# A hybrid decoder step on one core: routing tables on column groups, router logits turned, and the choice of experts one turn later

## What is computed

```python
lg = (t @ w_rg) + b_rg                       # 4 group logits of a token
gsel = argmax(lg);  pg_sel = softmax(lg)[gsel]
le = ((t @ w_re) + b_re).reshape(-1, 4, 8)   # 32 expert logits
le_sel = le[token, gsel]
top_v, top_i = top_k(le_sel, 2)
gate = softmax(top_v) * pg_sel
y[token] += sum_k gate_k * expert[8 * gsel + top_i_k](t)   # SwiGLU, 1024 -> 256 -> 1024, 32 experts
```

## Time and profile before

| what | us |
|---|---|
| median of 3 runs | 1306.74 |
| lowest, highest | 1301.86, 1311.63 |
| profiled execution, its own time | 1308.17 |
| its span in the trace | 1306.4 |
| PE busy, DVE busy, ACT busy | 1193.0, 702.5, 317.9 |
| mean DMA rate over the span | 165 GB/s of HBM traffic |

### The profile page before, as it was taken

How to read it: one execution, slowest core, us unless ns; L and a number is a source line. 1 busy time by engine, 2 the same in 40 slices (tenths; PEclk the granted TensorE clock), 3 DMA queues, 4 the chain that set the end, 5 groups by cost and what they waited for, 6 DMA issues and landing times.

```text
span 1306.4 us, 17526 instructions
## 1 busy us (share of the span) xinstructions
PE 1193.0 (91%) x6401; PEld 615.3 (47%) x6401; DVE 702.5 (54%) x2179; ACT 317.9 (24%) x916; POOL 143.0 (11%) x159
## 2 busy tenths in 40 slices
PE   7989879999999998797999999999867999999895
PEld 3435545555555545453555665555532334333231
DVE  1219789999999997431345544554552254212121
ACT  1133435345345356220111111121100110110100
POOL 0000000000000001000000000000001233333232
PEclk9998889999999998898999999999877999999898
DMA  8871000300000004266111011000766998999993
GB/s 318 307 236 31 1 1 25 127 35 33 33 1 33 25 1 167 97 240 254 33 48 49 1 49 48 33 8 25 282 243 237 402 335 312 329 380 384 391 352 60
DMA packets 48913, 194.88 MB, mean 149 GB/s; under 512 B 12240, under 2 KB 15094, under 8 KB 36515
## 3 DMA queue, kind: packets, MB, share of 16 engines
q1 hardware_dynamic: 37883, 173.79, 34.5%
q0 software_dynamic: 10368, 17.87, 5.8%
q10 hardware_dynamic: 576, 2.10, 0.4%
HBM read 172.60 MB, written 42.36 MB: 165 GB/s over the span
## 4 chain that ended last, share of the span: by engine, by line
PE 48%; DVE 5%; DMA 4%; issue 2%; ACT 0%; POOL 0%; SPq 0%; POOLq 0%; DVEq 0%
PE bank L1355 10%; PE bank L830 9%; PE bank L1301 8%; PE bank L1362 6%; PE bank L1279 3%; PE bank L1239 2%; PE bank L1344 2%; DMA W<-in_w_exp_down 1%; PE bank L1319 1%; PE bank L1103 1%; DMA W<-in_w_mo 1%; PE bank L1162 1%; DMA W<-in_cache_mem_k 1%; PE bank L836 1%; DVE G L1790 1%
## 5 line engine op out<-in xcount | busy, mean ns | idle before, releaser
L830 PE MATMUL bank<-W,G 128*128 128x512 f32 (+1 forms) x768 | 314.2, 565 | 3.8 <-DVE G L1790 3.0
L1846 DVE SCALAR_TENSOR_TENSOR W<-W,dwT 128x128 f32<-128x128 f32 (+1 forms) x1048 | 271.7, 335 | 0.0
L830 PEld LDWEIGHTS bank<-W,G 128*128 128x128 f32 x768 | 145.4, 193 | 150.6 <-issue 147.2
L1355 PE MATMUL bank<-W 128*32 128x512 f32 x1344 | 175.0, 604 | 1.7 <-DVE W L2345 1.7
L1301 PE MATMUL bank<-W 128*128 128x512 f32 x256 | 113.3, 595 | 0.2 <-DVE W L2217 0.2
L1103 PE MATMUL bank<-W 128*128 128x512 f32 x256 | 112.8, 599 | 0.0
L2345 DVE TENSOR_TENSOR W<-bank,cvec 128x512 f32<-128x512 f32 x48 | 31.0, 686 | 140.1 <-PE bank L1344 140.1
L703 POOL TENSOR_SCALAR st<-st 128x1 f32<-128x1 f32 (+3 forms) x40 | 7.9, 198 | 898.5 <-DVE st L1944 441.7
L1355 PEld LDWEIGHTS bank<-W 128*32 128x32 f32 x1344 | 49.6, 112 | 108.6 <-issue 106.2
L1362 PE MATMUL bank<-W 128*32 128x512 f32 x672 | 87.3, 595 | 1.5 <-ACT W L1737 0.9
L1103 PEld LDWEIGHTS bank<-W 128*128 128x128 f32 x256 | 48.5, 192 | 58.7 <-issue 58.5
(11 more groups left out here) (351 smaller groups left out, 1576.1 us busy)
## 6 DMA issues: line engine op xcount, KB each, us to landing
W<-in_w_exp_gate SPq DMA_DIRECT2D x27, 1024.0 KB, 12.5
W<-in_w_exp_up SPq DMA_DIRECT2D x27, 1024.0 KB, 15.1
W<-in_w_exp_down SPq DMA_DIRECT2D x27, 1024.0 KB, 18.9
W<-in_cache_mem_k SPq DMA_DIRECT2D x8, 1024.0 KB, 5.5
W<-in_cache_mem_v SPq DMA_DIRECT2D x8, 1024.0 KB, 8.0
W<-in_w_in SPq DMA_DIRECT2D x4, 1792.0 KB, 25.1
G<-in_w_exp_gate SPq DMA_DIRECT2D x5, 1024.0 KB, 15.0
G<-in_w_exp_up SPq DMA_DIRECT2D x5, 1024.0 KB, 18.1
```

What stands on the lines that cost most here:

```text
L830: mm = pe.matmul(bank[0:rows, at:at + hi - lo], HT[:, c, 0:rows], w[:, c, lo:hi], start=(c == 0), stop=(c == DC - 1))
L1355: mm = pe.matmul(B[2 + par][lo:hi, :], HG[par][:, c, lo:hi], WGU[u][:, :, c, :], start=(c == 0), stop=(c == DC - 1), skip_group_check=True)
L1846: dve.scalar_tensor_tensor(y, src, w, y, ALU.mult, ALU.add).then_inc(M["conv_tap"], 1)
```

## The change

The router swaps its operands: 36 weight columns stationary, H3 moving, even chunks on array columns 0 to 63 and odd ones on 64 to 127. ACT copies both halves to LT, one more matmul with two stacked identities (PAIR) adds and turns them, inside the output projection. `route_table` puts (token, gate) x (choice 0, 1) on four column groups of 32. The choice of tiles 0 to 6 moves into the next turn, between Z3 and the score maxima; that of tiles 7 and 8 stays. In the last turns gates are made after rows and tables, block 0's index is cast from PSUM directly and gathered first, and the first `gate_up` starts on half of its rows.

```diff
+            "lt_ready": ("kT_ready", NT), "rtt_done": ("kT_done", NT), "r_odds": ("kn_ready", NT),
@@ POOL
-            pool.wait_ge(M["route_ready"], 1)
             pool.wait_ge(M["z3_out"], 16 * NT)
             for n in range(2):
+                pool.wait_ge(M["route_ready"], n + 1)
                 gather(idx_i[:, BLOCKS[n]:BLOCKS[n] + 1], zg_in[n], ZG[n])
@@ PE
             def route_rank(s4):
+                if s4:
+                    pe.wait_ge(M["r_acc"], AFTER["r_acc"] + s4)
+                    pe.matmul(B[3][:, 0:NE], ones, RA, start=True, stop=False)
                 pe.wait_ge(M["r_hot"], AFTER["r_hot"] + s4 + 1)
+                pe.matmul(B[3][0:n4, 0:NE], tri[0:n4, 0:n4], RM[0:n4, :], start=(s4 == 0), stop=True)
+            def table_part(bank, c, n4):
+                for k in range(2):
+                    lo = 64 * c + NE * k
+                    mm = pe.matmul(bank[lo:lo + NE, 64:64 + POS], RQ[0:n4, k, c, :], RR[0:n4, k, :], start=True, stop=True)
+            def router(s3):
+                for c in range(DC):
+                    if c % 4 == 0:
+                        pe.wait_ge(M["h3_ready"], AFTER["h3_ready"] + 2 * s3 + c // 4 + 1)
+                    lo = 64 * (c % 2)
+                    mm = pe.matmul(B[1][lo:lo + 36, 0:n3], wr[:, c, :], H3[:, c, 0:n3], start=(c < 2), stop=(c >= DC - 2))
+                mm.then_inc(M["rt_done"], 1)
+            def router_turn(s3):
+                pe.wait_ge(M["lt_ready"], AFTER["lt_ready"] + s3 + 1)
+                pe.matmul(B[1][0:n3, 256:292], LT[0:100, 0:n3], PAIR[0:100, :], start=True, stop=True).then_inc(M["rtt_done"], 1)
...
                     for c in range(DC):
+                        if c == 3 and turned >= 0:
+                            router_turn(turned)
                         mm = pe.matmul(B[2 + half][0:n2, :], OT2[:, c, 0:n2], w_mo[:, c, 512 * half:512 * half + 512])
...
                 if 0 <= s3 < NT:
+                    router(s3)
                 if 0 < s2 < NT:
-                    output_half(1)
+                    output_half(1, s3)
+                elif s3 == NT - 1:
+                    route_table(s4)
+                    router_turn(s3)
...
-            gate_up(tiles_of(0), 0).then_inc(M["gu_done"], 1)
+            gate_up(tiles_of(0), 0, 2).then_inc(M["gu_done"], 1)
@@ ACT
-                if 0 <= s4:
+                if s4 >= NT - 2:
                     gate_exp(s4)
                 if 0 <= s3 < NT:
                     act.activation(SQ2[0:n3, :], XB(s3)[0:n3, :], ACT.Square)
+                if 0 <= s4 < NT - 2:
+                    gate_exp(s4)
...
+                if 0 <= s3 < NT:
+                    act.wait_ge(M["rt_done"], AFTER["rt_done"] + s3 + 1)
+                    act.activation(LT[0:36, 0:n3], B[1][0:36, 0:n3], ACT.Copy)
+                    act.activation(LT[64:100, 0:n3], B[1][64:100, 0:n3], ACT.Copy).then_inc(M["lt_ready"], 1)
                 if 2 <= s1 + 1 < NT:
                     nxt = s1 + 1
@@ DVE, route_hot
-                link(dve.tensor_scalar(lg[:, 0:NG], lg[:, 0:NG], top[:, 0:1], None, ALU.subtract))
-                link(dve.tensor_scalar(sel, lg[:, NG:NG + EPG], og[:, 0:1], None, ALU.mult))
-                for g in range(1, NG):
-                    link(dve.scalar_tensor_tensor(sel, lg[:, NG + EPG * g:NG + EPG * g + EPG], og[:, g:g + 1], sel, ALU.mult, ALU.add))
+                link(dve.tensor_tensor(own.rearrange("p (g e) -> p g e", g=NG), lg[:, NG:36].rearrange("p (g e) -> p g e", g=NG), bc(og, EPG, 2), ALU.mult))
+                link(dve.tensor_reduce(sel, own.rearrange("p (g e) -> p e g", g=NG), X, ALU.add))
...
                 dve.tensor_tensor(RM[0:n, :], RO[0:n, 0, :], RO[0:n, 1, :], ALU.add).then_inc(M["r_hot"], 1)
+                link(dve.tensor_scalar(lg[:, 0:NG], lg[:, 0:NG], top[:, 0:1], None, ALU.subtract))
+                dve.tensor_tensor(lg[:, 4:5], top[:, 2:3], top[:, 1:2], ALU.subtract).then_inc(M["r_odds"], 1)
@@ DVE, last tile in route_add
                     dve.wait_ge(M["r_place"], AFTER["r_place"] + 1)
+                    dve.tensor_copy(idx_i[0:64, 0:1], B[3][0:64, 320:321])
+                    dve.tensor_copy(idx_i[64:128, 0:1], B[3][0:64, 320 + NR:321 + NR]).then_inc(M["route_ready"], 1)
                     link(place_blocks(T_TOK, B[3]))
+                    dve.tensor_copy(idx_i[:, 1:NR], T_TOK[:, 1:NR]).then_inc(M["route_ready"], 1)
@@ DVE, the loop
+            dve.memset(LT, 0.0)
+            dve.tensor_tensor(PAIR, ident[:, 0:36], ident[:, 64:100], ALU.add)
             for it in range(1, NT + 3):
...
                     dve.tensor_scalar(by_row(Z3[0:n3, :], DC), XB(s3)[0:n3, :], st[0:n3, 41:42], None, ALU.mult)
+                if 0 <= s4 < NT - 2:
+                    route_hot(s4)
...
+                if s2 >= NT and s4 < NT - 1:
+                    route_shares(s4)
                 if s4 >= 0:
                     route_add(s4)
+                if s4 == NT - 1:
+                    route_shares(s4)
+                    last_gates()
...
+                if 0 <= s2 < NT:
+                    add_x2(s2, 0)
                 if 0 <= s3 < NT:
-                    dve.wait_ge(M["rt_done"], AFTER["rt_done"] + s3 + 1)
+                    dve.wait_ge(M["rtt_done"], AFTER["rtt_done"] + s3 + 1)
...
-                if 0 <= s3 < NT:
+                if NT - 2 <= s3 < NT:
                     route_hot(s3)
                 if 0 <= s2 < NT:
+                    add_x2(s2, 1)
```

More of the change, by code:

```diff
@@ L57 @@
 HALVES = [k for k, b in enumerate(COLUMNS) if len(b) == 2 and b[1][3] == 2]
+assert BLOCKS[0] == 0 and [c[2:4] for c in COLUMNS[0]] == [(0, 2), (0, 2)]
 QUARTER = [[k for k, b in enumerate(COLUMNS) if len(b) == 2 and b[1][2:4] == (q, 1)] for q in range(5)]
@@ L1179, in last_gates @@
                 pe.wait_ge(M["r_gates"], NT)
-                for k in range(2):
-                    mm = pe.matmul(B[6][NE:2 * NE, 0:POS], RQ[:, k, 1, :], RR[:, k, :], start=(k == 0), stop=(k == 1))
-                mm.then_inc(M["r_gtable"], 1)
+                table_part(B[6], 1, 128).then_inc(M["r_gtable"], 1)
             for it in range(1, NT + 3):
@@ L1334, in _ @@
             pe.wait_ge(M["r_tt"], AFTER["r_tt"] + 2)
-            place(B[6], NE)
+            place(B[6], 2 * NE)
             def turn_rows(n, u, rows_in, count, banks=(0, 1)):
@@ L1350, in tiles_of, with gate_up @@
                 return [(PART * k, PART * k + PART, u) for k, u in enumerate(slots)]
-            def gate_up(tiles, par):
+            def gate_up(tiles, par, upper=0):
                 for c in range(DC):
+                    if c == DC // 2 and upper:
+                        pe.wait_ge(M["hg_ready"], upper)
                     for lo, hi, u in tiles:
@@ L2026, in _, with add_x2 @@
                     add_x1(NT - 1)
+            def add_x2(s2, half):
+                n2, xr, cols = rows_of(s2), XB(s2), slice(512 * half, 512 * half + 512)
+                dve.wait_ge(M["mo_done"], AFTER["mo_done"] + 2 * s2 + half + 1)
+                dve.tensor_tensor(xr[0:n2, cols], B[2 + half][held(s2, half), :], xr[0:n2, cols], ALU.add).then_inc(M["x2_ready"], 1)
             def route_hot(s3):
@@ L2084, in route_rows @@
                     link(a)
+                dve.wait_ge(M["r_exp"], AFTER["r_exp"] + s4 + 1)
+                link(dve.tensor_scalar(part[:, 2:3], part[:, 1:2], 1.0, part[:, 0:1], ALU.add, ALU.mult))
+                link(dve.reciprocal(gate[:, 0:1], part[:, 2:3]))
+                link(dve.tensor_tensor(gate[:, 1:2], gate[:, 0:1], part[:, 1:2], ALU.mult))
+                link(dve.tensor_scalar(RQ[0:n, 0, 1, :], RO[0:n, 0, :], gate[:, 0:1], None, ALU.mult))
+                dve.tensor_scalar(RQ[0:n, 1, 1, :], RO[0:n, 1, :], gate[:, 1:2], None, ALU.mult).then_inc(M["r_gates"], 1)
                 link(dve.tensor_tensor(RP3[0:n], RO[0:n], bc(iota[0:n, 0:NE], 2, 1), ALU.mult))
```

88 lines of the change are left out of this document (45 added, 43 removed).

## The result

| | before | after |
|---|---|---|
| median, us | 1306.35 (10 runs) | 1295.28 (10 runs) |
| lowest | 1301.56 | 1293.13 |
| ratio, 95% interval | | 0.9918, 0.990 to 0.9937 |
| profiled execution, its span | 1308.17, 1306.4 | 1293.57, 1291.8 |

The account below looks back on a forecast made before the run. PE's program was taken to bound the full turns, with PE waiting only in turn 9 and the last chain. Full turns -6.0, turn 9 +3.0, last chain -5.9 gave -8.9 us: 1297.8 us from 1306.74, range 1289.0 to 1303.5.

Parts of the forecast that it names:

- Bound: PE's program limits full pipeline turns; DVE and ACT matter only where PE waits, in turn 9 and the last chain.
- Tables: Full turns on PE: four matmuls on four column groups take 0.5 us for 1.01, a gain of 0.5.
- Router: Full turns on PE: eight 128-column matmuls in four pairs take 1.0 us for 1.70, a gain of 0.7.
- Turning matmul: Inside the output projection on PE: two new records add 0.2 us a turn, bounds 0.1 and 0.45.
- The sum a turn: Tables, router and turning matmul together: -1.0 us a turn, -6.0 us over six turns.
- What hides the moved choice: Full turns on DVE: 4.6 us of choice fits the 6.42 us idle ahead of the first maximum, 1.8 to spare.
- Rival 4: Turns 3 to 8: norm_z waits for router, ACT, POOL, so DVE misses the second residual half; 1321 us, chance 0.03.
- Turn 9: No gap hides tile 6's choice, so softmax comes 3.5 us later: +3.0 us, bounds +1.5 and +5.
- Last chain: From the last tile's residual half to the first gate_up: -5.9 us, bounds -3 and -7; DVE, not the gather, ends the wait.
- The experts shift as a whole: The experts' stage starts earlier by the summed gain and keeps its length of 313 us.
- Rival 1: Experts: the long stall on late weights, 7.6 us together, goes as well; 1290.2 us, chance 0.16.
- Rivals 2 and 3: 2: short router pairs don't overlap, 1305.1 us, chance 0.08; 3: turn 9 and expert hand-over cost more, 1301.8, chance 0.16.

Follow-up runs that it names:

- e5: Changed kernel with all eight router matmuls on one column group instead of in pairs, one ACT copy instead of two: 1304.73 us, ratio 0.9985.
- e6: Changed kernel with the router as before (H3 stationary, 36 columns moved, no turning matmul, no ACT copies): 1300.80 us, ratio 0.9957.
- e2: Changed kernel with the choice of every tile back in the turn of its own router: 1310.72 us, ratio 1.0031.
- e9: As e2, but ACT takes the square of the next x ahead of its wait for the router: 1291.95 us, ratio 0.9891.
- e1: The changed kernel run again, unchanged: 1293.87 us, ratio 0.9909.
- e10: Changed kernel with ACT's square of the next x ahead of its wait for the router and the two copies: 1294.88 us, ratio 0.9910.
- e7: Changed kernel with block 0's index again made by one cast of all columns behind the place copies: 1296.00 us, ratio 0.9925.
- e3: Changed kernel with only tile 6's choice back in its own turn, turn 8: 1293.28 us, ratio 0.9906.
- e4: As e3, and DVE takes the first half of block 0's rows ahead of the gate place copies: 1293.01 us, ratio 0.9897.
- e11: e4 run again, unchanged, on another chip: 1292.68 us, ratio 0.9887.
- e12: e9 plus e4's edit, DVE taking the first half of block 0's rows ahead of the gate place copies: 1294.97 us, ratio 0.9923.
- e8: Changed kernel with the instructions from first maximum to the two one-hots run twice for the moved tiles: 1299.93 us, ratio 0.9938.

## Why the prediction was right, point by point

- **Bound.** PE's program in the full turns, waits only in turn 9 and the last chain: right; turns 3 to 8 all shortened by the same 0.80.
- **Tables**: 0.56 for 0.5. **Router**: 1.00, as taken. **Turning matmul**: I took 0.2 and put no price on what it and the router do to the groups beside them. Half 0 is 0.10 longer, half 1 0.24 for 0.2. The sum a turn is -0.8 for -1.0, -4.85 for -6.0 over all turns. The mis-sized term is the neighbours: 0.10 in half 0, 0.04 in half 1, with 0.06 in the tables, as measured. e5 and e6 show that the 0.10 comes with the 36-column form, paired (6.97) or not (6.96), against 6.87. The Trainium skill, TensorEngine Tiling (Array Packing), Key Properties, says that a change of tiling mode drains TensorE; 0.10 ahead of the router and, by 7.19 - 6.95 - 0.14 for the turning matmul itself, again 0.10 behind it are what a drain may cost here. No run separates it from filling and emptying of another kind.
- **What hides the moved choice.** Right in the kernel as changed: 4.5 us in the gap, 2.17 left. Rival 4's chain is there, with 1.9 us of spare time for 1.1. What I hadn't seen is that with ACT's new order this chain is the reason why the choice has to move at all: I put the logits on DVE at + 7.1 behind the router myself, and never added the 4.6 of the choice to it, which gives + 11.7 against the 8.25 at which the residual is due. e2 paid 17 us for this, and e9 took 15 of them away with ACT's old order.
- **Turn 9**: from 915.66 to PE's next work at 955.17 it is 39.5 us, before 922.40 to 960.46, 38.1: +1.45 for +3.0. The wait grew by 2.9 (3.5 forecast: the choice is 4.3 from its start to the maxima, as its first instruction overlaps Z3's end); tables -0.44, as said. The rest is the group behind the wait, 5.67 for 6.50 before. It scatters from 5.21 to 6.63 between kernels that do the same in it, so this 0.8 can't be counted as a gain of the change. That I took this stretch as "no longer after a longer wait" was right.
- **Last chain**, from the residual half at 954.43: logits at + 9.87 for + 12.21, -2.3 as forecast; first row instruction at + 14.95 for + 18.82, -3.9 as forecast; gather at + 20.17 for + 26.38, -6.2 for -6.3; gate_up at + 27.36 for + 33.68, -6.3 for -5.9. That DVE, not the gather, ends the wait was right in the trace of after and no more than a tie: in e1 and e10 the gather ends it, with gate_up at + 27.10 and + 27.36.
- **The experts shift as a whole**: wrong for the first block. It takes 9.85 us to the second gate_up for 11.95. In before PE had stood 3.97 us for the gather and then stayed at half clock for 5.9 us of the group, in after for 1.7. That the missing wait brought the clock back sooner is argued, not shown: e7, which brings 1.59 us of the wait back, has 10.98, but e5 and e6, without it, have 11.10 and 10.92, and the other changed kernels 9.70 to 10.56. The cause of this term stays open. From the second gate_up on nothing is gained. Rival 1 didn't come: the long stall is still there, 5.38 us for the 4.67 of the earlier trace rows.
```profile
1201.83 1.07 PE L1383 MATMUL bank<-G,W 128*32 128x512 f32 x3 [5.38 <-issue]
```
- **Sum**: -4.85 + 1.45 - 6.3 - 2.1 = -11.8 by the two traces, for -6.0 + 3.0 - 5.9 + 0 = -8.9. Two misses of opposite sign (turns +1.15, turn 9 -1.55) cancel nearly; 0.4 more came in the last chain, and what is left is the first block, which I had put at 0. The turns, turn 9 and the last chain came with the sign and the place that the mechanism gave them, but that the total lies within 3 us of the forecast is partly luck. Rivals 2 and 3 didn't come; e5 shows what 2 would have been: 1304.73, for 1305.1 worked out.

## What to carry to other kernels

A matmul group that uses few output columns pays when its halves run side by side on column groups; turning it for that is worth it only with the pairs, and some 0.1 us is lost in each neighbour. When a step is put into an in-order queue, follow what the steps ahead of it now wait for: one square behind another wait on ACT, with the choice still in DVE's queue behind it, came back as 2.3 us a turn on PE through POOL and DVE. Cut traces at fixed starts before comparing them: stages that repeat to 0.01 us stood here between two that scatter by 7 and 4 us.

## What I had not expected of the hardware

After a wait PE stays at the lower clock for a time that differs between executions of the same stretch. With waits of 4.4 us (before, e2, e3, e4, e9, e11, e12) the next group took 5.30 to 6.63 us, with waits of 7.3 us (after, e1, e5, e6, e7, e10) 5.21 to 6.20, and with 10.76 (e8) 5.37. A longer wait was no dearer. The clock fell at another moment of the wait each time, between 4.5 us before PE went on (e1) and 0.6 us after (e9), in e8 7.5 us before. An early fall came with an early return in e1, but in e4, where it fell only 0.8 us before PE went on, it was back as soon (6.0 us after, for 5.8 in e1). A gain of 1 to 3 us, as in e3, drowns in this. The first gate_up began at half clock in before, after, e5, e6 and e7 and left it after 5.9, 1.7, 3.9, 4.0 and 4.0 us; no run shows what sets these times.
